# Weight blocks laid out contiguously, cast once, and reread as bf16 by another queue

## What is computed

```python
x = x + 0.5 * swiglu(rmsnorm(x), ffn1_w_gate, ffn1_w_up, ffn1_w_down)      # hidden width 2816
h = rmsnorm(x)
glu_a, glu_b, q, k, v, g_conv, g_attn = split(h @ w_in)
conv_out = silu(layernorm(causal_depthwise_conv31(glu_a * sigmoid(glu_b)))) @ conv_w_proj
attn_out = sliding_window_gqa_sinks(rope(q), rope(k), v, sinks) @ attn_w_o # 16 heads of 64, 4 kv heads, window 128
x = x + (sigmoid(g_conv + b) * conv_out + sigmoid(g_attn + b) * attn_out) @ w_out
x = x + 0.5 * swiglu(rmsnorm(x), ffn2_w_gate, ffn2_w_up, ffn2_w_down)
out = rmsnorm_final(x)
```

## Time and profile before

| | us |
|---|---|
| median of 3 runs | 2008.72 |
| lowest, highest | 1988.82, 2282.69 |
| the profiled execution (slowest core) | 1984.8 |
| its eight cores | 1978.2 to 1984.8 |
| PE busy | 1785.2 (90%) |
| DVE, ACT, POOL busy | 663.6, 537.6, 465.6 |

### The profile page before, as it was taken

How to read it: one execution, slowest core, us unless ns; L and a number is a source line. 1 busy time by engine, 2 the same in 40 slices (tenths; PEclk the granted TensorE clock), 3 DMA queues, 4 the chain that set the end, 5 groups by cost and what they waited for, 6 DMA issues and landing times.

```text
span 1984.8 us, 25921 instructions; the slowest of 8 cores (1978.2 to 1984.8 us)
## 1 busy us (share of the span) xinstructions
PE 1785.2 (90%) x8762; PEld 804.9 (41%) x8930; DVE 663.6 (33%) x1150; ACT 537.6 (27%) x947; POOL 465.6 (23%) x569
## 2 busy tenths in 40 slices
PE   3899797999999898899999889799999989889997
PEld 1455442434444343343444334243444434334343
DVE  3322445331222246333132234533222124643212
ACT  2111316321221123622221121642122112362211
POOL 2113222112232313121232222211223231312111
PEclk9899898999999999999999989899999999999998
DMA  9899997799999998499999999669999999829987
GB/s 163 103 123 118 136 154 115 83 130 136 136 176 144 146 122 103 78 144 119 145 140 169 143 124 140 101 77 136 129 135 174 145 151 122 105 34 144 119 103 121
DMA packets 398350, 252.34 MB, mean 127 GB/s; under 512 B 9360, under 2 KB 385296, under 8 KB 398224
## 3 DMA queue, kind: packets, MB, share of 16 engines
q0 software_dynamic: 387792, 232.23, 96.1%
q1 hardware_dynamic: 10432, 18.46, 3.2%
HBM read 474.46 MB, written 8.39 MB: 243 GB/s over the span
## 4 chain that ended last, share of the span: by engine, by line
PE 75%; DMA 10%; DVE 6%; issue 4%; ACT 3%; POOL 1%; DVEq 0%; ACTq 0%; POOLq 0%
PE ps L299 45%; PE ps L367 14%; PE ps L522 6%; DMA wa<-wall 5%; DMA wd<-wd 3%; PE ps L667 3%; DMA ident_sb<-ident 2%; PE ps L635 2%; PE ps L639 2%; DVE tmp L647 1%; DVE tmp L429 1%; ACT sq L311 1%; DVE tmp L431 1%; DVE X L576 1%; DVE tmp L645 1%
## 5 line engine op out<-in xcount | busy, mean ns | idle before, releaser
L299 PE MATMUL ps<-xn,wa 128*128 128x512 bf16 x4055 | 943.8, 387 | 52.7 <-DVE xn L322 21.6
L299 PEld LDWEIGHTS ps<-xn,wa 128*128 128x128 bf16 x4160 | 407.6, 99 | 568.4 <-issue 109.3
L93 POOL DMA_DIRECT2D wa<-wall x322 | 282.6, 879 | 1070.7 <-PE ps L299 915.3
L367 PE MATMUL ps<-Hh,wd 128*128 128x512 bf16 x1373 | 318.2, 384 | 15.1 <-DMA wd<-wd 11.3
L343 DVE TENSOR_TENSOR Hh<-ps,tmp 128x512 bf16<-128x512 f32 x176 | 121.4, 691 | 485.8 <-PE ps L299 485.8
L341 ACT ACTIVATE tmp<-ps 128x512 f32<-128x512 f32 x176 | 105.1, 597 | 469.9 <-PE ps L299 469.8
L367 PEld LDWEIGHTS ps<-Hh,wd 128*128 128x128 bf16 x1408 | 136.8, 99 | 176.1 <-issue 27.9
L93 POOL DMA_DIRECT2D wd<-wd x176 | 123.8, 705 | 282.3 <-PE ps L367 282.3
L380 DVE SCALAR_TENSOR_TENSOR X<-ps,X 128x512 f32<-128x512 f32 x64 | 39.8, 684 | 259.2 <-PE ps L367 259.2
L522 PE MATMUL ps<-RR,wa 128*64 128x512 bf16 x1024 | 117.7, 379 | 1.4 <-DVE RR L512 1.4
L311 ACT ACTIVATE sq<-X 128x512 bf16<-128x512 f32 x96 | 54.7, 621 | 169.6 <-PE ps L313 75.1
(11 more groups left out here) (111 smaller groups left out, 1240.6 us busy)
## 6 DMA issues: line engine op xcount, KB each, us to landing
wa<-wall POOLq DMA_DIRECT2D x322, 512.0 KB, 10.8
wd<-wd POOLq DMA_DIRECT2D x176, 256.0 KB, 6.5
wa<-w POOLq DMA_DIRECT2D x32, 512.0 KB, 8.7
X<-xT SPq DMA_DIRECT2D x4, 2048.0 KB, 16.6
outT<-X SPq DMA_DIRECT2D x8, 1024.0 KB, 9.8
posi<-pos SPq DMA_DIRECT2D x4, 256.0 KB, 13.2
Xh<-xT SPq DMA_DIRECT2D x1, 512.0 KB, 7.0
masks_sb<-masks POOLq DMA_DIRECT2D x1, 384.0 KB, 36.1
```

What stands on the lines that cost most here:

```text
L93: inst = q.e.dma_start(out=out_ap, in_=in_ap)
L299: op(PE, lambda kc=kc: nc.tensor.matmul(pst[:, 0:N], lhsT=wslot[:, kc, sub * 128:(sub + 1) * 128], rhs=rhs_t[:, kc, 0:N], start=(kc == 0), ...
L367: op(PE, lambda pst=pst, dcl=dcl: nc.tensor.matmul(pst[:, 0:N], lhsT=wdt[:, sub, dcl * 128:(dcl + 1) * 128], rhs=Hh[:, fc, 0:N], start=(fc ...
```

## The change

The host lays each A block out as 128 x 2048 and each D block as 128 x 1024 floats, so that one partition's part of a block is one contiguous row, 8 KB or 4 KB. Two tensors `wac` and `wdc` in device memory hold bf16 copies. When a stream issues the load of a key for the first time, on POOL as before, it now also issues a store of the slot into the copy, on SP, which waits until the load has landed. When it issues a key again, it issues a plain bf16 load from the copy, on SP, which waits until the slot is free and the copy is written; POOL issues nothing then. Slots are reused only after the store that reads them is done. Each slot has three semaphores: load, store, reload. Every key recurs, so all blocks are stored. Sizes, slots, prefetch depth and the order of all else stay.

```diff
@@ class Stream
-    def __init__(self, q, slots, bufs, sems, keys, src, live=2):
+    def __init__(self, q, hq, slots, bufs, sems, ssems, hsems, keys, src, cache, live=2):
...
+        self.held = {}
+        self.uses = {}
+        for k in keys or ():
+            self.uses[k] = self.uses.get(k, 0) + 1
@@ _issue
-        dma(self.q, self.sems[s], self.slots[s], self.src(self.keys[j]), wr=(self.bufs[s],))
+        key = self.keys[j]
+        if key in self.held:
+            dma(self.hq, self.hsems[s], self.slots[s], self.cache(key), rd=(self.held[key],), wr=(self.bufs[s],))
+        else:
+            dma(self.q, self.sems[s], self.slots[s], self.src(key), wr=(self.bufs[s],))
+            if self.uses[key] > 1:
+                self.held[key] = Buf()
+                dma(self.hq, self.ssems[s], self.cache(key), self.slots[s], rd=(self.bufs[s],), wr=(self.held[key],))
@@ _build
-    wall_d = dt("wall", [D, NBLK_A * 256], F32, kind="ExternalInput").ap()
-    wd_d = dt("wd", [2 * DFF, D], F32, kind="ExternalInput").ap()
+    wall_d = dt("wall", [NBLK_A, 128, 2048], F32, kind="ExternalInput").ap()
+    wd_d = dt("wd", [44, 128, 1024], F32, kind="ExternalInput").ap()
+    wac_d = dt("wac", [NBLK_A + 8, 128, 2048], BF16, kind="Internal").ap()
+    wdc_d = dt("wdc", [44, 128, 1024], BF16, kind="Internal").ap()
...
-        SA = Stream(POOL, [w[:] for w in wa], wa_b, wa_s, None if rec is None else rec[0], asrc)
-        SD = Stream(POOL, [w[:] for w in wdd], wd_b, wd_s, None if rec is None else rec[1], dsrc, live=1)
+        SA = Stream(POOL, SP, [w[:] for w in wa], wa_b, wa_s, wa_ss, wa_hs, None if rec is None else rec[0], asrc, acache)
+        SD = Stream(POOL, SP, [w[:] for w in wdd], wd_b, wd_s, wd_ss, wd_hs, None if rec is None else rec[1], dsrc, dcache, live=1)
@@ _pack_shared
-    wall = np.ascontiguousarray(np.concatenate(blocks, axis=1))
+    wall = np.stack([np.asarray(b, f).reshape(8, 128, 256).transpose(1, 0, 2).reshape(128, 2048) for b in blocks], axis=0)
```

More of the change, by code:

```diff
@@ L102 @@
 class Stream:
[L103 removed]
+    def __init__(self, q, hq, slots, bufs, sems, ssems, hsems, keys, src, cache, live=2):
         self.live = live
         self.q, self.slots, self.bufs, self.sems, self.keys, self.src = q, slots, bufs, sems, keys, src
+        self.hq, self.ssems, self.hsems, self.cache = hq, ssems, hsems, cache
+        self.held = {}
+        self.uses = {}
+        for k in keys or ():
+            self.uses[k] = self.uses.get(k, 0) + 1
         self.depth = len(slots)
@@ L181, in _build @@
         wa_s = [mksem(f"s_wa{i}") for i in range(NA)]
+        wa_ss = [mksem(f"s_was{i}") for i in range(NA)]
+        wa_hs = [mksem(f"s_wah{i}") for i in range(NA)]
         ND = 7
@@ L184, in _build @@
         wd_s = [mksem(f"s_wd{i}") for i in range(ND)]
+        wd_ss = [mksem(f"s_wds{i}") for i in range(ND)]
+        wd_hs = [mksem(f"s_wdh{i}") for i in range(ND)]
         uT = sb("uT", [128, 8, 30 + NT], BF16); uT_b = [Buf() for _ in range(8)]
@@ L277, in late_setup, with acache, dix, dcache @@
                        rd=(ident_b, misc_b), wr=(sinkt_b,))
[L279 to L284, removed]
-        def asrc(key):
-            if key[0] == "W":
-                return w2_d[key[1]].rearrange("p (a b) -> p a b", a=8)
-            return ablk(key[1])
-        def dsrc(key):
-            return dblk(key[1], key[2], key[3])
-        SA = Stream(POOL, [w[:] for w in wa], wa_b, wa_s, None if rec is None else rec[0], asrc)
-        SD = Stream(POOL, [w[:] for w in wdd], wd_b, wd_s, None if rec is None else rec[1], dsrc, live=1)
+        def asrc(key):
+            t = w2_d[key[1]] if key[0] == "W" else wall_d[key[1]]
+            return t.rearrange("p (a b) -> p a b", a=8)
+        def acache(key):
+            t = wac_d[NBLK_A + key[1]] if key[0] == "W" else wac_d[key[1]]
+            return t.rearrange("p (a b) -> p a b", a=8)
+        def dix(key):
+            return (key[1] * 2 + key[2]) * 11 + key[3]
+        def dsrc(key):
+            return wd_d[dix(key)].rearrange("p (j c) -> p j c", j=2)
+        def dcache(key):
+            return wdc_d[dix(key)].rearrange("p (j c) -> p j c", j=2)
+        SA = Stream(POOL, SP, [w[:] for w in wa], wa_b, wa_s, wa_ss, wa_hs, None if rec is None else rec[0], asrc, acache)
+        SD = Stream(POOL, SP, [w[:] for w in wdd], wd_b, wd_s, wd_ss, wd_hs, None if rec is None else rec[1], dsrc, dcache, live=1)
         def proj(pst, pb, wslot, wbuf, sub, rhs_t, rhs_bufs, N):
@@ L802, in _pack_shared @@
     assert len(blocks) == NBLK_A
-    wall = np.ascontiguousarray(np.concatenate(blocks, axis=1))
-    wd = np.ascontiguousarray(np.concatenate([np.asarray(inp["ffn1_w_down"][0], f), np.asarray(inp["ffn2_w_down"][0], f)], axis=0))
+    wall = np.stack([np.asarray(b, f).reshape(8, 128, 256).transpose(1, 0, 2).reshape(128, 2048) for b in blocks], axis=0)
+    wall = np.ascontiguousarray(wall)
+    wd = np.stack([np.asarray(inp["ffn1_w_down"][0], f), np.asarray(inp["ffn2_w_down"][0], f)], axis=0)
+    wd = wd.reshape(2, 11, 2, 128, 2, 512).transpose(0, 4, 1, 3, 2, 5)
+    wd = np.ascontiguousarray(wd.reshape(44, 128, 1024))
     gate_b = np.asarray(inp["gate_b"][0], f)
```

## The result

The changed kernel is slower: 2072.01 us (median of 4 runs) against 2010.17 (4 runs), a ratio of 1.035, 95% interval 1.026 to 1.045. The profiled executions say the same: 2071.4 against 1984.8, 86.6 us more.

A forecast was written before the change was run, and what follows sets the result against it. PE, busy 1785.2 of 1984.8 us, was taken as the bound, so only its waits or clock matter. Terms -25 + 21 + 18 + 1 + 5 + 4 = +24 gave 2009 profiled, 2020 for the runs; range 1975 to 2075.

The forecast's parts named there:

- Gain in tiles 1 to 3: Tiles 1 to 3: lighter bf16 reloads remove PE's weight waits and the low clock behind them; gain 25 us, 18 to 30.
- Start: Start of tile 0: Xh and X wait on SP's queue behind eleven stores; loss 21 us, 9 to 41.
- Tile ends: Three tile ends: next X queues behind reloads on SP, PE's gap grows and low clock follows; loss 18 us, 0 to 45.
- Positions: Positions load on SP is passed by stores and reloads, but rope's positions still arrive 40 us ahead of use.
- Tile 0, loads and stores: Tile 0's dense stretch: at 394 GB/s loads and stores together lose nothing; 5 us taken, bounds 0 and 41.
- the halo's burst: Halo mixer's ten short blocks in tile 0: added stores and block 22's reload behind a store; loss 4 us, 0 to 8.
- rival 2: DMA engines or HBM cannot carry tile 0, from 336 GB/s down; at 305 the term is 41, total 2056 us; chance 0.22.

The follow-up runs named there:

- early_x: Changed kernel with Xh, X and positions issued before the streams, next X and positions before the attention; stores and reloads kept: ratio 1.025 to the kernel before, 2044 us.
- contig_only: Changed kernel with the contiguous layout alone, every block cast by POOL each time, no store or reload: ratio 1.001 to the kernel before, profiled span 1975.7 us.
- old_layout: Changed kernel with the layout undone (rows of 1 KB and 2 KB), stores and reloads kept: span 2096.1 us on the slowest core, no ratio measured.
- store_sbuf: Changed kernel without reloads, each block stored once, to scratch in the core's own memory: gate/up 102.7 us against 132.4 with stores to device memory; no ratio.

## Why the prediction was wrong, by its own steps

**Gain in tiles 1 to 3: right in size, wrong in cause.** 25 us were forecast. Without the late X (early_x) tiles 1 to 3 win 29.2 against core 4 before and 22.5 against the quickest core, with it 18.7. I gave the gain to reading bf16; contig_only shows that contiguity wins it all, and old_layout that bf16 reads would win it as well. The second half of the change was bought for a gain that the first half had already made.

**Start: the mechanism was right, the size half.** The term was 21, measured 40.2. Three steps were mis-sized, and they make up the difference: Xh left SP at 43.9 where I took 33, took 13.3 us where I took 6, and X took 11.3 where I took 9, together 20.5. The first is again the rate: with 12.1 MB at 394 GB/s the stores were to be out by 34; my high bound of 43, at 305 to 328, was the right one. What the sum lacked is a second loss that hides behind this one: in contig_only, with no store, the start costs 21.9 us, since full contiguous packets stand beside X's small ones. I had read contiguity as cheaper for all who share the engines.
**Tile ends.** 18 us were forecast for three. Measured against early_x: 13.7 in tile 0 and 10.5 in tiles 1 to 3, 24.2; of the 10.5 the two gaps explain 7.3, and the rest is within what cores differ by. The step from a gap of 5 us to a low clock behind it failed: the gap came as forecast (5.14 and 4.69 us in tiles 1 and 2), but the down projection behind it ran in the same 19.84 us as before, at a granted clock of 1.00 and 0.99; behind tile 0's 15.2 us it was 0.87. In tile 0 X took 17.5 us, for the engines were busy with the saturated stream; the forecast had them idle.

**Positions: the step failed.** "Rope's positions still arrive 40 us ahead of their use": true of the tables, but DVE computes them ahead of X's update L400, in its own queue, and PE's second half waits for that. 6.7 us in tile 0. What stands behind a moved load on the consumer's queue counts, not when its result is used.

**Tile 0, loads and stores: the wrong row.** The term was 5 with bounds of 0 and 41, and 4 more for the halo's burst; early_x shows 42.8 for both, and in the changed kernel about 45 are left in tile 0 once the start, the positions (6.7) and the late X (13.7) are taken off. The step that failed is "the nearest are the contiguous reads", 394 GB/s: that was a row of 2 us. Contiguous reads alone ran at 340 over 30 us, and reads and writes together at 321 over 126, under the 336 that rival 2 named as its threshold. Rival 2 was the right one, but its 41 us were not: they belong to 305 GB/s, and at 321 its own sum gives 30. Gate/up and down 1 show 23.4 + 3.2 us in early_x; the rest is 3.8 in down 0, for which the sum had no term, and 12.4 in the mixers, which hold both the halo's burst, forecast 4, and the start of the dense stretch. The mixers lose 10.8 in the changed kernel, 7.4 in store_sbuf and 21.9 in old_layout; a part of it is the reload of block 22 that waits for a store (4.9 us in the changed kernel).

**Sum.** Forecast +24; measured +86.6: 40.2 at the start (21 forecast), 24.2 for X at the tile ends (18), 6.7 positions (0), about 43 for the stores (9 with the halo), less about 29 (25); these make 85. The start and the stores came out at their upper bounds (41, and 41 + 8), and a late X within its own (0 to 45). The two slips in the working, 3.7 MB for ten stores that are 3.9 and a mean of 2.3 for 2.2, change nothing. The measured 2072 lies inside the stated range, but the forecast was "no change" and the kernel is clearly slower. That rival 2's 2056 comes so near is partly luck: its stores were sized at the wrong rate, and it too had the start 19 us short and the positions at nothing.

## What to carry to other kernels

Before a copy is built to save traffic, run the cheaper half alone: here the layout removed every weight wait of tiles 1 to 3, and the copy could only cost. When a transfer goes to another queue, list what that queue issues for others (inputs, positions, outputs) and put those first; and when packets grow, look at who sends small ones beside them, and give that load a place in front in the same ring. A stream that just fits does not bear a second stream of half its size: here all stores cost gate/up 23.4 us and half of them nothing there. Take the rate for such a sum from a stretch as long as the one you plan, not from 2 us. And two causes that delay the same load can hide each other: take each away alone.

## What the runs showed of the hardware that I had not expected

- Beside full 8 KB casting packets a load of 1024 packets of 512 B took 25.2 us, against 7.0 beside 1 KB ones; the queues shared the engines by packets (985 to 1033), not by bytes (3.09 to 0.52 MB).
- With all eight cores running, a core exchanged 321 to 325 GB/s with the device memory, reads and writes together, over 90 us and more, and 340 with contiguous casting reads alone, over 30; with rows of 1 KB the full engines read 286. Once the stores stayed in the core, the 16 engines moved 263 GB/s (written) in place of 213, and a casting load landed in 9.2 us in place of 21.7.
- The DMA share read 1.03 and 1.00 in that pair: it does not tell engines that are the limit from engines that wait for the memory.
- Halving the stores brought their cost in gate/up from 23.4 us to none (111.3 to 87.6).
- A gap of 5 us in PE's work was followed by matmuls at full pace at the tile ends, while gaps of 4 us in the earlier trace rows were followed by a low clock, and one of 15.2 us by 0.87. Why was not settled.
